# Modulation vectors of layers 1 to 3 as row sums on VectorE instead of matrix-vector products on TensorE

## The reference

```python
cond = silu(c)                                    # (B, D), D = 1024
for layer in range(4):
    mod = cond @ ada_w[layer] + ada_b[layer]      # (B, 6D): the modulation vector
    sh1, sc1, g1, sh2, sc2, g2 = split(mod, 6)
    h = rms_norm(x, norm_mix_g) * (1 + sc1) + sh1
    y = short_conv_mixer(h) if layer % 2 == 0 else mlstm_mixer(h)
    x = x + (1 + g1) * y
    h = rms_norm(x, norm_ffn_g) * (1 + sc2) + sh2
    u = causal_dwconv(h @ w_up, conv_w, width 3) + conv_b      # 2 * 2816 channels
    x = x + (1 + g2) * ((silu(u_gate) * u_value) @ w_down)
return rms_norm(x, final_norm_g)
```

## Time and profile before

| | us |
|---|---|
| median of three runs (lowest, highest) | 2952.57 (2952.46, 2977.8) |
| the profiled execution | 2951.92 |
| its span on core 4 | 2950.3 |
| spans of the eight cores | 2939.3 to 2950.3 |
| TensorE busy | 2849.4 (97%) |
| VectorE busy | 1989.7 (67%) |
| ScalarE busy | 1210.7 (41%) |
| GpSimd busy | 951.9 (32%) |

### The profile page before, as it was taken

One profiled execution on the slowest core, in us unless ns is written; L12 is line 12 of the kernel. 1 busy time (PEld: TensorE's weight loads), 2 busy tenths in 40 slices (PEclk: granted clock), 3 DMA queues, 4 the chain that ended last, 5 costly groups with the idle time before them and its releaser, 6 DMA issues.

```text
span 2950.3 us, 45095 instructions; the slowest of 8 cores (2939.3 to 2950.3 us)
## 1 busy us (share of the span) xinstructions
PE 2849.4 (97%) x15410; PEld 1358.4 (46%) x15696; DVE 1989.7 (67%) x2679; ACT 1210.7 (41%) x1910; POOL 951.9 (32%) x861
## 2 busy tenths in 40 slices
PE   3999999999999999999999999999999999999998
PEld 1444444444454544444444444444445454444443
DVE  1767676787565667678766767668766565766873
ACT  3323452453444345335322335425535352542551
POOL 1110352353252434316311014405405262441440
PEclk9999999999999999999999999999999999999999
DMA  9887678677834357667675548576671616457533
GB/s 178 141 110 103 96 101 110 98 107 101 115 45 72 58 86 115 93 104 108 101 96 71 83 70 121 83 111 103 101 105 30 101 25 95 75 78 108 80 58 114
DMA packets 290800, 276.48 MB, mean 94 GB/s; under 512 B 9616, under 2 KB 284304, under 8 KB 290576
## 3 DMA queue, kind: packets, MB, share of 16 engines
q0 software_dynamic: 283232, 256.00, 60.2%
q1 hardware_dynamic: 7344, 17.58, 1.9%
HBM read 521.15 MB, written 8.39 MB: 179 GB/s over the span
## 4 chain that ended last, share of the span: by engine, by line
PE 93%; DMA 2%; DVE 1%; issue 1%; ACT 1%; POOL 0%; DVEq 0%; SPq 0%; ACTq 0%; POOLq 0%
PE ps L228 93%; DMA ring<-ada_w 1%; ACT work L188 1%; DMA x_sb<-xT 1%; PE ps L237 1%; DVE work L191 1%; DMA ring<-ml_w_in 0%; DVE x_sb L201 0%; DVE work L201 0%; SPq L242 0%; DVEq L261 0%; POOL work L215 0%; POOL ring L242 0%; POOL work L194 0%; ACT L188 0%
## 5 line engine op out<-in xcount | busy, mean ns | idle before, releaser
L228 PE MATMUL ps<-h_sb,ring 128*128 128x512 bf16 x8000 | 1776.0, 380 | 22.0 <-ACT h_sb L188 8.0
L228 PEld LDWEIGHTS ps<-h_sb,ring 128*128 128x128 bf16 x8192 | 795.1, 98 | 959.3 <-issue 19.8
L201 DVE SCALAR_TENSOR_TENSOR work<-ps,params_sb,work 128x1023 bf16<-128x1023 f32 x704 | 901.9, 1281 | 279.1 <-ACT halo_u L188 160.6
L228 PE MATMUL ps<-work,ring 128*128 128x512 bf16 x3637 | 807.3, 379 | 12.3 <-DVE work L191 4.6
L188 ACT ACTIVATE work<-ps,params_sb 128x1024 bf16<-128x1024 f32 x352 | 423.5, 1203 | 702.1 <-PE ps L228 702.0
L194 POOL TENSOR_TENSOR work<-work 128x1024 bf16<-128x1024 bf16 (+2 forms) x288 | 511.9, 1791 | 391.0 <-ACT work L188 360.7
L201 DVE SCALAR_TENSOR_TENSOR x_sb<-ps,mods,x_sb 128x512 f32<-128x512 f32 x480 | 359.1, 750 | 359.3 <-PE ps L228 349.0
L228 PEld LDWEIGHTS ps<-work,ring 128*128 128x128 bf16 x3712 | 361.4, 98 | 440.8 <-issue 9.6
L188 ACT ACTIVATE h_sb<-work,mods 128x512 bf16<-128x512 f32 x192 | 138.1, 722 | 417.6 <-DVE work L201 401.1
L188 ACT ACTIVATE work<-ps 128x512 bf16<-128x512 f32 (+3 forms) x352 | 178.5, 520 | 231.4 <-PE ps L228 220.3
L188 ACT ACTIVATE work<-work 128x1024 bf16<-128x1024 bf16 (+4 forms) x224 | 211.3, 943 | 110.3 <-DVE work L191 90.8
(11 more groups left out here) (67 smaller groups left out, 1107.8 us busy)
## 6 DMA issues: line engine op xcount, KB each, us to landing
ring<-ffn_w_up POOLq DMA_DIRECT2D x80, 1024.0 KB, 12.0
ring<-ada_w POOLq DMA_DIRECT2D x48, 1024.0 KB, 10.9
ring<-ffn_w_down POOLq DMA_DIRECT2D x30, 1024.0 KB, 10.1
ring<-ml_w_in POOLq DMA_DIRECT2D x24, 1024.0 KB, 9.4
ring<-sc_w_in POOLq DMA_DIRECT2D x32, 512.0 KB, 9.3
ring<-ffn_w_down POOLq DMA_DIRECT2D x16, 768.0 KB, 8.9
ring<-sc_w_in POOLq DMA_DIRECT2D x8, 1024.0 KB, 11.1
ring<-sc_w_out POOLq DMA_DIRECT2D x8, 1024.0 KB, 9.4
```

The costliest lines, as they stand in the source:

```text
L201: return self.op("dve", lambda e: e.scalar_tensor_tensor(out=out, in0=in0, scalar=scalar, in1=in1, op0=op0, op1=op1), reads, [out])
L228: return self.op("pe", lambda e: e.matmul(out, lhsT=lhsT, rhs=rhs, start=start, stop=stop), [lhsT, rhs], [out], mark=mark)
```

## The change

- A second copy of the modulation weights, `ada_t`, is an input, with rows and columns exchanged. A block of it is 512 rows (entries of the vector) of 1024 terms and goes into a ring slot as 128 partitions by four rows of 1024. It has the same bytes as before.
- silu(c) is kept on all 128 partitions as `cond_b` (1024 in bf16). Its source `c_rows` (128x1024 float32) is loaded by the sync engine's queue at the start, behind x, and one ScalarE instruction makes `cond_b` at the head of the first MLP stage. To make room, the norm's accumulator `acc_v` now shares the bytes of the second half of `rs_v`.
- For layers 1 to 3, `consume_dve` takes the place of `consume` inside `ffn_phase`: four scalar_tensor_tensor instructions of 128x1024 bf16, in place in the ring slot, each with an accumulated row sum that goes straight into `mods`. They are put into a list, and `ada_tick` takes two of them after the matmuls of each channel block of the up projection (ahead of ScalarE's and VectorE's work on it), or two after each group of the down projection. After the fourth the slot is given back. While the list isn't empty the next `use_block` holds one slot.
- Layer 0, and blocks 10 and 11 of layer 1, stay on TensorE. So 34 of the 48 blocks change engine.
- In the mLSTM stages chunk 3 is transposed earlier in the last step (before `step_num(7)`), and the four hooks take banks by age instead of the fixed ones.

```diff
+            if kc < 0:
+                dst = ring[:, s, :, :].rearrange("p k n -> p (k n)").rearrange("p (m k) -> p m k", m=4)
+                S.dma("pool", dst, src, ring_sem[s], writes=[ring[:, s, :, :]])
...
+        def wblock_rows(w_ap, r0):
+            src = w_ap[r0:r0 + 512, :].rearrange("(m p) k -> p m k", p=128)
+            blocks.append((src, -1, 1024))
+            return len(blocks) - 1
...
+            def consume_dve(j, bi):
+                slot = use_block(bi).rearrange("p k n -> p (k n)").rearrange("p (m k) -> p m k", m=4)
+                def one(m):
+                    q = 4 * j + m
+                    S.stt_acc(slot[:, m, :], slot[:, m, :], cond_b, mods[:, slot_l, q:q + 1])
+                    if m == 3:
+                        done_block(bi)
+                return [lambda m=m: one(m) for m in range(4)]
...
+            ada_q = []
+            def ada_tick():
+                for _ in range(2):
+                    if ada_q:
+                        ada_q.pop(0)()
...
                 for (kind, i, ncols, bi), extra in seq[:nup]:
-                    slot = use_block(bi)
+                    slot = use_block(bi, hold=1 if ada_q else 0)
...
                             S.group(ps[:, pr + t2, :], wchunks(slot, m), hcols(hf, hs))
+                        ada_tick()
                         acc = accv[:, m, :] if kind == "v" else accg[:, jj % 3, :]
...
                             xupdate(pb_ap, mc, hf, t2, gate)
+                            ada_tick()
...
-                    pt = ps[:, bank, :].bitcast(BF16)
+                    pt = (next_bank() if bank is None else ps[:, bank, :]).bitcast(BF16)
...
                         o_group()
+                        step_t(3)
                     step_num(c)
...
-                    if c >= 4:
+                    if 4 <= c < 7:
                         step_t(c - 4)
...
-                hooks = [(lambda c=c: step_t(c, (0, 1, 2, 3)[c - 4])) for c in range(4, 8)]
+                hooks = [(lambda c=c: step_t(c, None)) for c in range(4, 8)]
```

More of the change, by code:

```diff
@@ L277, in build_program @@
     dr["ada_w"] = nc.dram_tensor("ada_w", [nl, D, 6 * D], F32, kind="ExternalInput").ap()
+    dr["ada_t"] = nc.dram_tensor("ada_t", [nl, 6 * D, D], F32, kind="ExternalInput").ap()
+    dr["c_rows"] = nc.dram_tensor("c_rows", [128, D], F32, kind="ExternalInput").ap()
     dr["ffn_w_up"] = nc.dram_tensor("ffn_w_up", [nl, D, 2 * DFF], F32, kind="ExternalInput").ap()
@@ L348, in build_program @@
         tmpn_v = cv_([2, 512], F32)
-        acc_v = cv_([512], F32)
+        acc_v = rs_v[:, 1, :]
         ssum_v = cv_([2, 512], BF16)
+        cond_b = cv_([D], BF16)
         cv_ = Carver(0)
@@ L391, in build_program @@
         st_sem = S.dma_sem("st")
+        crow_sem = S.dma_sem("crow")
         S.dma("sp", params[:, :], dr["params"], misc_sem)
@@ L404, in build_program @@
         S.act(condT[:, :], params[:, P_C:P_C + 8], AF.Silu)
+        c_tmp = view(work, 45056, [D], F32)
+        S.dma("sp", c_tmp, dr["c_rows"], crow_sem)
         blocks = []
@@ L412, in issue_next @@
             s = i % NS
-            if isinstance(src, tuple):
+            if kc < 0:
+                dst = ring[:, s, :, :].rearrange("p k n -> p (k n)").rearrange("p (m k) -> p m k", m=4)
+                S.dma("pool", dst, src, ring_sem[s], writes=[ring[:, s, :, :]])
+            elif isinstance(src, tuple):
                 for n, part in enumerate(src):
@@ L475, in ada_parts, with reg @@
             psa = ps[:, 4, 448:496]
-            def reg(j):
+            on_dve = li > 0
+            def reg(j, pe=False):
+                if on_dve and not pe:
+                    return wblock_rows(dr["ada_t"][li], j * 512)
                 return wblock(dr["ada_w"][li], 0, D, j * 512, 512)
+            def consume_dve(j, bi):
[6 more added lines that the diff above has]
+                return [lambda m=m: one(m) for m in range(4)]
             def consume(j, bi):
@@ L485, in consume, with finalize @@
                 done_block(bi)
-            def finalize(lo, hi):
+            def finalize(lo, hi, pe=not on_dve):
                 md = mods[:, slot_l, lo:hi]
-                S.tt(md, psa[:, lo:hi], params[:, pb + P_ADAB + lo:pb + P_ADAB + hi], ALU.add)
+                S.tt(md, psa[:, lo:hi] if pe else md, params[:, pb + P_ADAB + lo:pb + P_ADAB + hi], ALU.add)
                 for (o_sc, o_g, pg) in ((8, 16, P_NMG), (32, 40, P_NFG)):
@@ L496, in finalize @@
                         S.ts(a_g, a_g, 1.0, None, ALU.add)
-            return reg, consume, finalize
+            return reg, consume, finalize, consume_dve
         ada0 = ada_parts(0)
@@ L767, in ada_step @@
                 a, aj, abi = extra
-                a[1](aj, abi)
                 if a is ada0:
+                    a[1](aj, abi)
                     if aj == 11:
                         a[2](40, 48)
-                elif li == 0:
+                    return
+                while ada_q:
+                    ada_q.pop(0)()
+                ada_q.extend(a[3](aj, abi))
+                if li == 0:
                     if aj in (3, 9):
-                        a[2](*((0, 16) if aj == 3 else (16, 40)))
+                        ada_q.append(lambda: a[2](*((0, 16) if aj == 3 else (16, 40))))
                 elif aj in (5, 11):
-                    a[2](24 * (aj // 6), 24 * (aj // 6) + 24)
+                    ada_q.append(lambda: a[2](24 * (aj // 6), 24 * (aj // 6) + 24))
             def run():
                 early = []
+                if li == 0 and hf == 0:
+                    S.act(cond_b, c_tmp, AF.Silu)
                 if tail:
@@ L888, in mlstm_phase @@
             if late:
-                b_late.append(late[0](10))
+                b_late.append(late[0](10, True))
             b_k = wblock(w_in, 0, D, 512, 512)
             if late:
-                b_late.append(late[0](11))
+                b_late.append(late[0](11, True))
             b_v = [wblock(w_in, 0, D, 1024 + 512 * i, 512) for i in range(2)]
@@ L946, in run @@
                     late[1](11, b_late[1])
-                    late[2](40, 48)
+                    late[2](40, 48, True)
                 v_slot = [use_block(b_v[0]), use_block(b_v[1], hold=1)]
@@ L1178, in _launch @@
         "ada_w": np.ascontiguousarray(inp["ada_w"][l0:l1]),
+        "ada_t": np.ascontiguousarray(np.asarray(inp["ada_w"][l0:l1]).transpose(0, 2, 1)),
         "ffn_w_up": np.ascontiguousarray(inp["ffn_w_up"][l0:l1]),
@@ L1192, in _launch @@
         m["params"] = params_list[b]
+        m["c_rows"] = np.ascontiguousarray(np.broadcast_to(np.asarray(inp["c"][b], np.float32)[None, :], (128, D)))
         in_maps.append(m)
```

## The result

The changed kernel takes 2966.69 us (median of 20 executions), against 2953.47 us for the kernel before (also 20): a ratio of 1.004, 95% interval 1.0026 to 1.0053. It is slower by some 13 us. The forecast was 61 us slower. The direction was right, the size was not. 13 us lie under the 1% that I had called the limit of what can be told; the interval of this comparison is narrower than that and leaves out a ratio of 1, so a small loss is shown. The profiled execution took 2965.81 us with a span of 2964.1 us on core 5, 13.8 us more than before.

A forecast was written before the change was run, and what follows sets the result against it. TensorE was taken to bound the kernel. Stalls of 90.6 us plus 5.3 for the accumulator, less 27.2 removed and 6.9 for small edits, gave +61.8: 3014 us (chance 0.5), range 2955 to 3034.

The forecast's parts named there:

- What bounds the kernel: TensorE holds 93% of the chain that ended last, so a removed piece of its work is worth its full price.
- what is removed: 34 modulation blocks leave TensorE at 0.80 us each, 27.2 us; 12 lie in down projections, 22 in up projections.
- the down projections: Row sums of 5.34 us a block fit VectorE's room of about 12 us; 12 blocks gain their full 9.6 us.
- The small edits: mLSTM stages: bank waits of 8.6 us go, eight transposes now show for 1.7; together -6.9 us, other edits 0.
- The ring slot: Up projections: the slot returns later but its load lands in time; counted 0, at most 1 us at each of 22 spots.
- What VectorE gets: Each row sum takes VectorE 1.335 us, 5.34 us a block and 182 us in all, coming in lumps.
- GpSimd in the way: Up projections: row sums with two SBUF inputs wait for GpSimd, first and between the first two; stalls total 90.6 us.
- (a): Rival: GpSimd doesn't get in between two row sums; stalls 57.4 us, +28.6 us, 2981 us; chance 0.2.
- (d): Rival: the ring slot comes late, or a third wait for GpSimd; above 3034 us; chance 0.08.
- (b): Rival: no sharing between VectorE and GpSimd for row sums; stalls 38.3 us, +9.5 us, 2962 us; chance 0.1.
- (c): Rival: row sums short enough, 0.73 us each at the bf16 double rate; no stall, 34.1 us gained, 2918 us; chance 0.12.
- The signs I named: TensorE's VectorE waits 80 or 90 us, two a spot; row sums up to 3.4 us; mLSTM waits gone; none in down projections.

The follow-up runs named there:

- e2: The changed kernel, but the up projections' modulation blocks stay on TensorE and only the 12 in down projections are row sums: 2933.8 us against 2950.3 for the kernel before.
- e1: The kernel before with the mLSTM edits alone (chunk 3 transposed earlier, hooks' banks by age): 2943.1 us against 2950.3, ratio 0.9974.
- e6: The changed kernel with silu(c) read from PSUM in up projections and one row sum after each channel block: 2933.1 us against 2948.2 for the kernel before.
- e4: The changed kernel with one row sum after each channel block instead of two: 2950.9 us against 2950.3 for the kernel before, ratio 1.0004.
- e5: The changed kernel, row sums still in pairs, but silu(c) read from PSUM in up projections: 2941.49 us against 2950.3 for the kernel before, ratio 0.9971.
- e9: e5 with the modulation block's slot and the next value block's given back only after the next gate block's first channel block: 2940.0 us against 2948.2 for the kernel before.
- e7: The changed kernel with all four row sums after the first channel block, inputs in SBUF: 2989.4 us against 2948.2 for the kernel before.

## Why the prediction was right or wrong

**What bounds the kernel, what is removed, the down projections: right.** e2 gave -16.5 us for 9.6 + 6.9, and the six down projections of the profile after are 9.3 us shorter.

**The small edits: right.** -7.2 us in e1 for -6.9, with the 1.7 us of uncovered transposes as forecast.

**The ring slot: right for pairs** (no wait on `ffn_w_up` in the profile after), with less room than I wrote. Four channel blocks instead of two before it comes back make 15.6 us of waits on the slowest core in e6 and 17.8 in e4, and as little as 3.1 and 0.9 on others.

**The step that failed is "What VectorE gets", with the two sizes in "GpSimd in the way".** The mechanism stood: two stalls a spot, at the pairs of v0 and v1, by VectorE's end on v1. The terms in them came out at 47.2 us for 95.9:

- *The row sum, 1.335 us, and the accumulator, 0.06.* I took the taps' pace and added the accumulator. Measured is a step of 1.145 with the accumulator in it. The 2.67 us that I halved hold the 1.38 us before a second tap that adds to the first's result, and the last tap's whole length; the row sums don't depend on each other, and only their step counts. Four times 0.25 us at 22 spots: 22 us too much. The accumulator's read does exist, with 0.083 us, and is hidden. The Trainium skill ("VectorE: DVE Perf Modes", Two Vector instructions with no wait between them) has an instruction with an accumulated output as two instructions; the trace agrees on the count, 136 reads for 136 row sums. No price of the second shows here: the step of 1.145 us with it is no longer than the 1.20 from a tap without one to the next instruction.
- *The first wait in half 1, 1.2 us.* GpSimd's multiplication is waited out by the two-column addition, which was in the count of VectorE's work already, and after it the row sum is in turn: 12 x 1.2 = 14.4 us too much. In half 0 the wait was 0.45 for 0.5.
- *GpSimd's turn in half 1, 2.0 us.* It is an instruction of 128x512 with 1.06, at nine spots, and there is none at the three first spots: 9 x 0.94 + 3 x 2.0 = 14.5 us too much, against which those three had some 1.4 us each more of a backlog ahead, 4.1 us. In half 0 it was 1.06 for 1.14.

22 + 14.4 + 14.5 - 4.1 = 46.8, and small terms in half 0 (8 x 0.08 + 10 x 0.05 = 1.1) make 47.9 of the 48.7 us. The rest is not assigned. The first bullet is seen in every run with row sums and the turns are isolated by e5; that the first row sum of half 1 doesn't wait because the two-column addition has already waited is read from the trace, and no run takes that addition away.

**The turns themselves: right.** e5 took away the row sums' sharing, with VectorE's work in the same order, and 23 us went. The Trainium skill ("SBUF — State Buffer", Who interferes with whom) says that a VectorE instruction with two inputs in SBUF contends with a GpSimd instruction that reads SBUF and one with a single SBUF input doesn't; the runs agree, 2.28 us at most with both in SBUF (2.75 in e4) and 1.218 with one in PSUM.

**The rivals.** The measured time lies in my range by luck: the range reached down to 2955 to take in a rival, not because I thought my terms could be twice too large. (a) and (d) didn't happen. (b), no sharing, with its +9.5 us is nearest to the measured +13, but for a wrong reason: it had the long row sums without the turns. e5 is what (b) describes, and it is some 9 us *faster* than the kernel before, because of the shorter step. (c) put the point from which the row sums pay in half 0 at 1.18 us; the step of 1.145 is under it, and in e5 the stall there is 0.60 us for 0.80 saved. The rate doubled by narrow types, which (c) rested on, didn't come: 1.21 us for 1024 elements.

**The signs I named.** Two waits a spot: yes, at 20 of 22. No wait in down projections, mLSTM waits gone: yes. 80 to 90 us: no, 40.5 in up projections, and those of half 1 under the name L191. Longer in half 1: by 0.07 us only. Row sums up to 3.4 us: no, 2.28. GpSimd's 128x1024 multiplications lengthened: hardly, from 2.126 to 2.157 us in the mean of 176; it was its 128x512 instructions that grew (below).

## What to carry to other kernels

Price a new instruction by the distance between starts in a row of its own kind, not by its length or by the pace of instructions that wait for each other's results, and where a small difference between work given and time saved decides, hold the sum open until that row is measured. When work is handed in pieces to an engine that also frees buffers, three limits stand against each other: how much stands ahead of a buffer's reader, how long a borrowed slot is held, and whose turn it is where two engines both read SBUF; here one operand in PSUM took away the last, and the order two, one, one balanced the other two, for 0.8%. Look at the same wait on several cores before it is called the cause: in e4 and e9 the slowest core showed one that its neighbours hardly had. Between two engines with a backlog, look for what has already waited: the next in the queue then doesn't.

## What the runs showed of the hardware

- The read of VectorE's accumulator is an instruction of its own, 0.075 to 0.089 us, inside the 1.145 us from one row sum's start to the next. Two taps of almost the same size take 2.58 (412.14 to 414.72): 1.38 where the second adds to the first's result (1.37 to 1.39 for such pairs in the trace before), and 1.20 to the row sum behind them.
- With both inputs in SBUF, VectorE's and GpSimd's instructions took turns: one GpSimd instruction between the first and second row sum at 17 of 22 spots, never two, at a price of 1.06 us for 128x512. A longer row of turns isn't shown: in e7, with four row sums in line, GpSimd was held up by a load. GpSimd pays as well. Its group of such additions before (this fence) and after (the next), busy us and mean ns:

```profile
L194 POOL TENSOR_TENSOR work<-work 128x512 f32<-128x512 f32 x96 | 121.4, 1265 | 63.8 <-ACT work L188 63.8
```

```profile
L194 POOL TENSOR_TENSOR work<-work 128x512 f32<-128x512 f32 x96 | 132.7, 1382 | 81.9 <-ACT work L188 81.9
```

- With some stalls of 1.9 us and more TensorE's granted clock fell to 0.5 for 3.4 us, which costs some 1.7 us (7 of 22 stalls on core 3 in e7, 11.9 us); the changed kernel's 42 stalls in up projections, of at most 1.6 us, brought no such stretch on any of the eight cores.
